# Summing the expert rows of a mixture-of-experts layer: eight plain gathers and VectorE additions in place of accumulating gathers, and a new order of the first expert loads

## The reference, cut to what matters

```python
for l in range(DEPTH):                       # DEPTH = 2
    h = rmsnorm(x, norm1_g[l])
    q, k, v, qi, ki, wi, pool_in, conv_in = split_columns(h @ w_in[l])
    y_a = dsa_attention(...); y_b = pool_mixer(...); y_c = conformer_conv(...)
    x = x + concat([y_a, y_b, y_c]) @ w_out[l]
    h2 = rmsnorm(x, norm2_g[l])
    x = x + hier_moe(h2, ...)                # each token: 2 of 16 experts
return rmsnorm(x, final_g)

# hier_moe, for one expert e and the tokens that chose it:
#   act = silu(h2 @ w_gate[e]) * (h2 @ w_up[e]) * gate
#   y  += act @ w_down[e]
```

## Time and profile before

| what | us |
|---|---|
| median of three runs | 1162.16 |
| lowest and highest | 1161.47, 1162.86 |
| the profiled execution | 1170.0 |
| its span, first to last instruction | 1168.1 |
| TensorE busy | 1101.5 (94%) |
| VectorE busy | 533.9 (46%) |
| ScalarE busy | 298.9 (26%) |
| GpSimd busy | 207.3 (18%) |

### The profile page before, as it was taken

How to read it: one execution, slowest core, us unless ns; L and a number is a source line. 1 busy time by engine, 2 the same in 40 slices (tenths; PEclk the granted TensorE clock), 3 DMA queues, 4 the chain that set the end, 5 groups by cost and what they waited for, 6 DMA issues and landing times. The chain is left out here.

```text
span 1168.1 us, 27573 instructions
## 1 busy us (share of the span) xinstructions
PE 1101.5 (94%) x12160; PEld 865.0 (74%) x12160; DVE 533.9 (46%) x1237; ACT 298.9 (26%) x572; POOL 207.3 (18%) x277
## 2 busy tenths in 40 slices
PE   8999998999899999999589999989989999999994
PEld 7875885688689877896378668847876888789952
DVE  4997997435211201110269889964452112111114
ACT  5234338523000010000242342484320000100002
POOL 3300000000332333322200000000012333233231
PEclk9999999999999999999889999999999999999997
DMA  9742211127989999999923222111289899999996
GB/s 339 239 149 86 77 37 55 37 90 265 401 313 357 402 402 402 402 405 370 293 118 111 70 74 90 36 38 54 90 326 401 292 395 404 403 402 402 405 330 171
DMA packets 87655, 284.27 MB, mean 243 GB/s; under 512 B 11888, under 2 KB 11952, under 8 KB 87520
## 3 DMA queue, kind: packets, MB, share of 16 engines
q1 hardware_dynamic: 71040, 237.60, 53.6%
q0 software_dynamic: 16480, 44.75, 12.1%
HBM read 259.23 MB, written 23.07 MB: 242 GB/s over the span
## 5 line engine op out<-in xcount | busy, mean ns | idle before, releaser
L1707 DVE SCALAR_TENSOR_TENSOR arena<-ps,gslot,arena 128x128 f32<-128x128 f32 x96 | 27.8, 345 | 407.7 <-ACT arena L1170 407.7
L791 PE MATMUL ps<-raw,arena 128*32 128x256 f32 x2880 | 168.4, 385 | 7.0 <-DVE arena L1700 5.9
L791 PE MATMUL ps<-arena 128*32 128x256 f32 x2784 | 162.2, 379 | 1.2 <-issue 1.1
L791 PEld LDWEIGHTS ps<-raw,arena 128*32 128x32 f32 x2880 | 129.3, 111 | 41.3 <-issue 9.9
L791 PEld LDWEIGHTS ps<-arena 128*32 128x32 f32 x2784 | 132.4, 110 | 25.7 <-issue 7.2
L578 POOL DMA_INDIRECT gain<-h_rows,tab x96 | 93.9, 979 | 273.1 <-DVE arena L1700 222.4
L420 PE MATMUL ps<-a_hi,w_hi 128*128 128x512 f32 (+1 forms) x304 | 122.0, 401 | 2.8 <-DVE w_lo L401 2.1
L421 PE MATMUL ps<-a_lo,w_hi 128*128 128x512 f32 (+1 forms) x304 | 119.4, 393 | 0.0
L422 PE MATMUL ps<-a_hi,w_lo 128*128 128x512 f32 (+1 forms) x304 | 119.2, 392 | 0.0
L1170 ACT ACTIVATE arena<-ps 128x384 f32<-128x384 f32 x32 | 15.7, 490 | 341.7 <-PE ps L791 341.7
L396 ACT ACTIVATE w_hi<-raw 128x1024 fp32r<-128x1024 f32 (+1 forms) x64 | 65.3, 1023 | 141.4 <-PE ps L422 130.6
(11 more groups left out here) (235 smaller groups left out, 1503.7 us busy)
## 6 DMA issues: line engine op xcount, KB each, us to landing
raw<-in_w_gu SPq DMA_DIRECT2D x120, 512.0 KB
arena<-in_w_gu SPq DMA_DIRECT2D x116, 512.0 KB
raw<-in_w_dn SPq DMA_DIRECT2D x64, 512.0 KB
arena<-in_w_dn SPq DMA_DIRECT2D x52, 512.0 KB
raw<-in_w_in SPq DMA_DIRECT2D x40, 512.0 KB
y_rows<-arena POOLq DMA_DIRECT2D x112, 96.0 KB
deep<-in_w_gu SPq DMA_DIRECT2D x20, 512.0 KB, 12.7
raw<-in_w_out SPq DMA_DIRECT2D x16, 512.0 KB
```

Of the source, the lines that this page charges most:

```text
L791: mm = T.matmul(o, rows, piece[:, :, c * P:(c + 1) * P], start=b == 0, stop=b == 7)
L1707: ins = V.scalar_tensor_tensor(out=slu[:, s, :], in0=hidden(e, 1)[:, s, :], scalar=gslot[:, s, e:e + 1], in1=slu[:, s, :], op0=ALU.mult, o ...
```

## The change

Three things are changed. The eight gathers are all plain, in the order of the token tiles, into eight buffers (`late_rows`: `acc`, `sq`, two pieces of `deep`, `ysb`'s place, `pTs[0]`, `hrow`'s last row, and the place of the gathered expert rows); the sixth waits until the gate and up product of expert 15 is done (`LATE_FREE`). VectorE adds all eight: four ahead of `last_y(l, 1)` and four behind it. Of the four splits for the next layer, one stays there, and three go between the `norm_lo` of the next layer. SP now issues expert pieces 8 to 13 into slots 12 to 17, after the first `w_out` piece is used, and after them pieces 14 to 17 into slots 8 to 11; the wait for `x_mixed` is gone.

```diff
-FIRST_SLOTS = (*range(RAW + 6), *range(RING_E, FIRST), *range(RAW + 6, RING_E))
+RAW_EARLY = 8
+FIRST_SLOTS = (*range(RAW_EARLY), *range(RAW, RAW + 6), *range(RAW_EARLY, RAW), *range(RING_E, FIRST), *range(RAW + 6, RING_E))
...
-LATE = 2
+LO_AHEAD = 1
...
-        late_rows = [ar(A_L, D), ar(A_V, D)]
...
+        late_rows = [ar(A_ACC, D), ar(A_SQ, D), *(deep[:, d].rearrange("p a n -> p (a n)") for d in (3, 7)),
+                     ar(A_L, D), ar(A_PT, D), hrow[:, TT - 1, :], ar(A_V, D)]
+        LATE_FREE = 5
...
-                load_expert_pieces(0, RAW)
-                sp.wait_ge(x_mixed, 8 * (l + 1))
-                load_expert_pieces(RAW, RAW + SIDE_MIX)
+                load_expert_pieces(0, RAW_EARLY)
+                sp.wait_ge(w_used, l * PIECES_L + PIECES_IN + 1)
+                load_expert_pieces(RAW_EARLY, RAW + SIDE_MIX)
                 sp.wait_ge(w_used, l * PIECES_L + PIECES_MIX)
...
-                for tt, k in ((2, 0), (3, 0), (0, 0), (0, 1), (1, 0), (2, 1), (3, 1), (1, 1)):
-                    at = bass.IndirectOffsetOnAxis(ap=yidx[:, 0, k, tt:tt + 1], axis=0)
-                    if k and tt < LATE:
-                        if tt:
+                for tt in range(TT):
+                    for k in range(TOPE):
+                        q = TOPE * tt + k
+                        if q == LATE_FREE:
                             pool.wait_ge(w_used, (l + 1) * PIECES_L - 8)
-                        pool.indirect_dma_start(late_rows[tt], None, yd, at).then_inc(yc_in[tt], 16)
-                        continue
-                    if k:
-                        pool.wait_ge(yc_in[tt], 32 * l + 16)
-                    pool.indirect_dma_start(x[:, tt, :], None, yd, at, compute_op=ALU.add).then_inc(yc_in[tt], 16)
+                        pool.indirect_dma_start(late_rows[q], None, yd,
+                                                bass.IndirectOffsetOnAxis(ap=yidx[:, 0, k, tt:tt + 1], axis=0)).then_inc(yc_in[tt], 16)
...
                 ve.wait_ge(yc_in[tt], 32 * (l + 1))
-                V.tensor_tensor(x[:, tt, :], late_rows[tt], x[:, tt, :], ALU.add).then_inc(late_add, 1)
+                for k in range(TOPE):
+                    ve.wait_ge(late_add, TOPE * (TT * l + tt) + k)
+                    V.tensor_tensor(x[:, tt, :], late_rows[TOPE * tt + k], x[:, tt, :], ALU.add).then_inc(late_add, 1)
...
                     norm_lo(2 * l, (2 * j, 2 * j + 1))
                     if l == 0:
                         lo(ve, n0 + j)
+                    elif j + LO_AHEAD < AHEAD:
+                        lo(ve, n0 + j + LO_AHEAD)
...
                     if l + 1 < DEPTH:
-                        for j in range(AHEAD):
+                        for j in range(LO_AHEAD):
                             lo(ve, (l + 1) * PIECES_L + j)
...
                 with ve.Else():
+                    add_late(l, 0)
+                    add_late(l, 1)
                     last_y(l, 1)
-                    for tt in range(LATE):
-                        add_late(l, tt)
+                    add_late(l, 2)
+                    add_late(l, 3)
                     next_lo()
```

More of the change, by code:

```diff
@@ L615, in _ @@
                 with pool.If(extra > 0):
-                    pool.wait_ge(late_add, LATE * (l + 1))
+                    pool.wait_ge(late_add, TT * TOPE * (l + 1))
                     pool.wait_ge(over[l].tab_step, TABLES)
@@ L1458, in add_late @@
                 ve.wait_ge(yc_in[tt], 32 * (l + 1))
-                V.tensor_tensor(x[:, tt, :], late_rows[tt], x[:, tt, :], ALU.add).then_inc(late_add, 1)
+                for k in range(TOPE):
+                    ve.wait_ge(late_add, TOPE * (TT * l + tt) + k)
+                    V.tensor_tensor(x[:, tt, :], late_rows[TOPE * tt + k], x[:, tt, :], ALU.add).then_inc(late_add, 1)
             def sum_ready(l, tt):
-                if tt < LATE:
-                    ve.wait_ge(late_add, LATE * l + tt + 1)
-                else:
-                    ve.wait_ge(yc_in[tt], 32 * (l + 1))
+                ve.wait_ge(late_add, TOPE * (TT * l + tt + 1))
                 ve.wait_ge(ysum_ready, TT * l + tt + 1)
```

## The result

The changed kernel takes 1156.83 us (median of 8 runs, 1154.38 to 1160.03) against 1162.78 us (1161.47 to 1166.71, 8 runs) of the kernel before on the same chip: ratio 0.9944, 95% interval [0.9928, 0.9960], a gain of 6.0 us by the medians (interval of the ratio: 4.7 to 8.4). Forecast were 13.8 us and 1148.4. The direction was right, the size was not: less than half of the gain is there. A later set of runs gave 1157.31 us and 0.9940 [0.9919, 0.9960].

What follows compares the result with a forecast made beforehand. TensorE, busy 94%, had one long wait of 15.4 us between the layers, set by the eighth gather's landing. Gains of 11.9 us (layer 0) and 1.9 (layer 1), 13.8, took 1162.2 to 1148.4 us; range 1143.5 to 1157.

Steps and rivals of the forecast that it cites:

- Gathers: End of each layer: plain gathers take 1.3 us each instead of 2.5, issued 1.28 us apart; last landing 563 to 566.
- The rival of slow gathers: End of each layer: plain gathers are no faster than 207 GB/s; gain only 7.4 us, 1154.8 us; chance 10%.
- Branch: VectorE behind the first `last_y` of each layer: getting through the branch costs 2 us.
- late code: Rival: code behind VectorE's branch comes 5.6 and 7.0 us late; gain only 5.2 us, 1157.0 us; chance 18%.
- Layer 0: End of layer 0: additions and splits let the first sum start at 573.6 instead of 585.46, 11.9 us gained.
- Everything behind it moves along: Behind layer 0's first sum: norm, transposes and projection come as much sooner as the sum, with nothing lost.
- Layer 1: End of layer 1: sums start at 1152.2 instead of 1154.06, a gain of 1.9 us.
- Splits between the `norm_lo`: Next layer's norm: three moved splits cost nothing there; without that cover 3.6 us.
- Loads: Six expert pieces issued about 40 us sooner: given no gain, as the full ring gives it back as idle DMA time.

Runs made afterwards that it cites:

- e1: Changed kernel with VectorE's register load and branch moved ahead of the first `last_y` of a layer; 1149.75 us, ratio 0.9870 to the kernel before.
- e2: Changed kernel with the If part of VectorE's branch cut to the instructions shared with the Else part (16 in layer 0); 1152.05 us, ratio 0.9883.
- e7: e1 with the last `w_lo` split also moved out of the Else part, ahead of the first `norm_lo`; 1149.59 us, ratio 0.9877.
- e10: e7 with 10, 8 and 4 idle products on TensorE in its waits ahead of the transposes; 1150.78 us, ratio 0.9892.
- e6: Kernel before with one small write of zeros on VectorE as first instruction behind the branch in both layers; single execution, 1164.62 us.
- e17: The kernel of e6, unchanged, in another execution; 1163.05 us.
- e8: Changed kernel with the four `w_lo` splits back in one place ahead of the first sum; 1160.97 us, ratio 0.9976.
- e5: Changed kernel with all eight additions behind `last_y(l, 1)`, none ahead of it; 1157.78 us, ratio 0.9946.
- e4: Kernel before with only the new order of the first expert loads; 1163.62 us, ratio 0.9996.
- e3: Changed kernel with the old order of the first expert loads and the wait for `x_mixed` back; 1154.36 us, ratio 0.9921.

## Why the prediction was wrong

- **Gathers: rate and issues right, the last landing too early.** 387 GB/s in 550 to 552 at a DMA share of 1.02, issues 1.26 us apart. The rival of slow gathers is out: e1 adds the first rows 8.65 us behind the first issue. But the last tile's rows were forecast 12.6 to 15.6 us behind the first issue, and where VectorE came early enough to wait for them (e1, e2, e7, e10) they landed 18.2 to 19.7 us behind it. In the changed kernel nothing waits for them.
- **Branch: the step that failed.** "I take 2 us, nearer to POOL's row". It was 6.18 in layer 0 and 5.37 in layer 1. I had both ends of the range and took the wrong row to be near. POOL's 0.67 us tells of POOL's program, in which the branch jumps over 40 instructions and not over some 250 (the prediction's "about a hundred rows" was too low as well); VectorE's own 7.03 us and ScalarE's 7.07 us "<-issue" were closer to the place. By the rival's sum ("late code", 18%) the forecast was 1157.0, and 1156.8 came. Its mechanism is shown by e1, e2 and the packets; that its number fits so well is luck, as it had 8.3 us won in layer 0 and 3.1 lost in layer 1, where the profiles have 6.4 won and at most 0.9 lost. What it did not say is that the kernel before had the wait in layer 1 only (e6, e17), so that in layer 0 it came with the change.
- **Layer 0: 11.9 us forecast ahead of the first sum, 7.88 measured.** The 4.2 us of the branch explain it. The rest of the chain is as counted: four additions, split, four additions, split take 12.3 us (561.34 to 573.64), forecast 12.5.
- **Behind the first sum: 0 forecast, 0.7 to 1.5 us lost.** "Everything behind it moves along" did not hold. Before, TensorE's granted clock fell to 0.5 after its wait of 15.4 us and was back at 1.00 for the last transposes:

```profile
592.00:598.00 6.00, 4.19 (x34) 3.76 (x34) 3.31 (x9) 3.31 (x7) 0.00 (x0) 1.00 0.06 25
```

Now it falls twice. It is 0.52 in 566 to 572, behind the 4.2 us of waiting inside the sums, 1.00 in 574 to 578, and 0.50 in 580 to 586, just where the transposes stand. The 16 products of L663, which took 1.95 us before, take 2.83:

```profile
580.76 4.28 PE L662 MATMUL ps<-cst,arena 128*128 128x128 f32 x18 [1.30 <-DVE arena L1434]
584.84 2.83 PE L663 MATMUL ps<-arena,x_sb 128*128 128x128 f32 x16
```

What brings the second fall is not isolated. e8 has the same wait inside the sums (4.0 us) and e5 has none of it, and both are back at 12.65 us with the last transposes at 1.00; both wait longer just ahead of the first sum (3.4 and 7.5 us against 0.3). And it isn't the change alone: the kernel before with a marker took 12.66 us in one execution (e6) and 13.61 in the other (e17).

- **Layer 1: 1.9 us forecast, between 0.9 lost and 1.0 won.** 3.4 us more of branch than assumed take it.
- **Splits between the `norm_lo`: right for the first sum** (3.0 to 3.4 us, count 3.5), not for the whole: by the profiles of e8 a part of it is given back behind the sum.
- **Loads: right.** Nothing by e4. The dip of the DMA engines is still there, earlier and not clearly longer, and so is TensorE's wait for a down piece, 3.32 us now (2.0 in e3, 1.4 in e4):

```profile
908.00:912.00 4.00, 4.00 (x80) 3.39 (x71) 1.56 (x4) 0.00 (x0) 1.94 (x2) 1.00 0.18 60
912.00:916.00 4.00, 4.00 (x79) 3.10 (x80) 0.00 (x0) 0.80 (x1) 2.41 (x5) 1.00 0.43 96
936.00:1100.00 164.00, 160.62 (x2927) 142.21 (x2922) 27.28 (x82) 14.39 (x23) 49.86 (x68) 1.00 1.03 403
```

```profile
1099.82 5.77 PE L829 MATMUL ps<-arena,pw 128*32 128x256 f32 x52 [3.32 <-DMA arena<-in_w_dn]
```

Together: 13.8 forecast, less 4.2 and 3.4 for the branch and 1.5 behind the sum, is 4.7; 5.6 are in the stretches and 6.0 in the medians. The branch is the term that was mis-sized: 2 us a layer in the sum, 6.18 and 5.37 in the trace.

## What to carry to other kernels

Work that is put right behind a runtime branch pays for the way to its code, even if the branch itself was free before; it was free only while the engine waited there for something else. Put the branch where the engine waits anyway, or keep the part that is jumped over short: on top of the change the first brought 7.1 us by the medians, more than the change itself, and the second 4.8 (in a kernel without VectorE's overflow part). And when an unshown cost has two bounds, take the row of the same engine in the same place, not the nearest value on another engine.

## What the runs showed of the hardware

- A taken branch over 250 instructions cost VectorE 4.7 to 6.6 us in layer 0 of the changed kernel and its variants and 2.8 to 5.5 in layer 1; over the short part of 16, 0.4 and 0.5. Each of the long waits of the table has two or three packets of the instruction queue in it, the short ones none.
- With the DMA engines nearly idle (share 0.02 to 0.08) the same wait was 2.8 to 3.1 us long.
- Nearly the same branch (243 and 239 instructions) cost 0.8 to 1.9 us in one layer of the marked kernel and 5.7 to 5.9 in the other.
- Gathers without an add moved 387 GB/s in a window in which nine tenths of the traffic was theirs, against 207 with one.
- The first stretch of the kernel, up to the router's transposes of layer 0, lasts 261 or 265 us from execution to execution. A difference of spans between two profiles has to be cleared of that first.
